# Four edits in one kernel: y stored from another queue, a new order of the first loads, a last block in two passes, and banded scores on row halves

## The chip, the cores and the metric

The kernel runs on one core of a Trainium2 chip. The time is the device time of one execution in microseconds (us). The engines of the core work in parallel, each through its own list of instructions, and meet at semaphores: TensorE (PE in the profile, its weight loads PEld), VectorE (DVE), ScalarE (ACT), GpSimd (POOL), and SyncE (SP), which here only issues transfers. PE's results land in eight PSUM banks; everything else is in SBUF.

## What is computed

A sequence of 512 tokens with 2048 channels goes through three layers, all in 32-bit floating point:

```python
# layer 1: forgetting attention, 32 heads of 64, full causal
p = rmsnorm(x) @ fox_w_in ; y = softmax(q k^T * scale + c_i - c_j) v ; x += (y * silu(gate)) @ fox_w_out
# layer 2: sliding window attention, 32 query heads, 4 key heads, window 128, one sink per head
p = rmsnorm(x) @ swa_w_in ; y = softmax over a band of two 128-key blocks ; x += (y * silu(gate)) @ swa_w_out
x = rmsnorm(x, final_g)
# layer 3: half of the channels through an RWKV-7 scan (16 heads of 64), half through HGRN-2 (8 heads of 128)
proj = x @ w_in_2 ; y = concat(o_rwkv, o_hgrn) @ w_out_2
out = layer_norm(ALPHA * x + y, ln_w, ln_b)
```

In the band, block b of 128 queries sees the 128 keys of its own block and the 128 of the block before it; block 0 has only its own.

## The kernel before

**Products.** Every large product is a list of blocks b of 512 output columns. A block needs 16 tiles of 128 input channels (kt); the weights come in slots of two kt, 8 slots in a block, 512 KB each. `products` (L243) issues for each kt and each of four banks j three matmuls (high x high, low x high, high x low, since each number is split in two parts), so a block is 192 matmuls of 512 columns. SP loads slot s into one of `NR` = 5 buffers once `w_free` says that slot s-4 has begun; ACT makes the high part (`split_act`, L523) into one of `NH` = 3 buffers, DVE the low part (`split_dve`, L674), both two slots ahead of PE. DVE takes a finished bank out and counts up `bank_free[j]`, for which the next block waits at its first kt.

**Side work.** The rest of the layers is woven between the matmuls of `products` at numbered points (4 kt + j, 64 in a block). The other engines hold the matching pieces in the same order, slot by slot, behind the split of the slot.

**The start.** SP issues six small constants (L1886), on which PE, ACT and DVE all wait, then weights and the transposed input xt in turn (L890, L891). POOL issues at once the gains, `w_f`, small parameters, cos and sin, and 1 MB of x (L899 to L906). ACT and DVE wait for four of POOL's parameters, and for xt in pairs of slots (`x_in`, 32 counts for two transfers).

**Sliding window scores.** `swa_scores` (L423) runs in each of 64 steps (4 groups g of 16 steps k; k is a head pair and a query block b = k % 4). For each of the two heads e it issues one fp32 matmul of the 128 rows of q of both heads against `kzs[:, e]`, in which the rows of the other head are zero, and then adds the mask by a bf16 matmul (`identb`, `maskb`). Both heads of a step share one bank, and steps alternate between two (`S_BANK`). DVE takes the row maxima of both heads in one reduction (L759), then L760 and L762; ACT takes the exponentials (L559) and that of the sink (L563); DVE divides (L768 to L770); PE turns the result (`swa_turn`, L449) in the next step and multiplies by v (`swa_values`, L460) in the one after. Steps are 5.8 points apart, in the last group 4 (`swa_step_at`).

**RWKV and HGRN units.** Layer 3 has 8 RWKV and 8 HGRN units. The product blocks alternate between them, and the side work of a unit runs under the blocks behind it. `hg_take` (L1623) takes HGRN unit h out of the banks into `hqs, hf, hi_, hz`; the y of the unit before it, in `hz_split` and `hkdtm_split` of the same memory, must by then have been stored in DRAM (`y_h_st`), and its last step is the subtraction L1711 (`y_h_lo`). POOL makes both stores (L1832, L1833), in a list sorted by the place at which each is due, together with the stores of RWKV's y (L1828, L1829) and with `sub_inverses` (L1789 to L1811): the inverses of 16 x 16 blocks by way of DRAM, at whose end POOL waits until `xt` has landed. In that list the stores of HGRN units 3, 4 and 5 stand behind `sub_inverses` of RWKV units 5, 6 and 7. After the list POOL loads all of y back for the last product (L1841, L1842), and the last product's first matmul waits for it.

**The end.** The last product (`out`, four blocks n of 512 output channels over four token tiles t, one bank each) is followed on DVE by the sum (L1717), `bn_stats` (L1721), `bn_aggr` (L1753) and the reciprocal root for all four tiles, then tile by tile the scaling on ACT (L1462, 2048 columns), the product with `ln_w` and the sum with `ln_b` on DVE (L1760, L1761), and a 1 MB store by SP (L1773).

## Time and profile before

| | us |
|---|---|
| median of 3 runs | 3324.41 |
| lowest and highest | 3318.13, 3325.99 |
| the profiled execution | 3318.51 |
| its span in the trace | 3316.7 |
| PE busy (15418 matmuls) | 3090.8 (93%) |
| DVE busy | 1656.3 (50%) |
| ACT busy | 1177.3 (35%) |
| POOL busy | 207.3 (6%) |

PE is busy for 93% of the span, and the chain that ended last runs over PE for 81% of it. The kernel can become faster where PE waits, where its clock is granted at the lower level, at the two ends where PE has no work, or where PE has less to do. The granted clock of the whole execution is 0.973 of full speed. A start in the trace is the instruction's own; a matmul's end is modelled, so the cost of a few matmuls is read from starts: from the last large matmul ahead of them to the second one behind them, less the two steps of 0.227 us that these take anyway.

### The profile page before, as it was taken

The numbers are of one execution on the slowest core, as the hardware profiler recorded it, in microseconds if no ns is written. First come the engines' busy times: TensorE is split into PE (matmuls) and PEld (weight loads), VectorE is DVE, ScalarE is ACT, GpSimd is POOL, SyncE is SP. The second block draws the span as 40 slices with busy tenths as digits, with TensorE's granted clock in tenths as the row PEclk, the third lists the DMA queues.
The fourth block names the chain that finished last, engine by engine and source line by source line (L and its number), as shares of the span: only waits on it lengthen the run. The fifth ranks groups of instructions, "written<-read, shape, count | busy, mean of one in ns | idle before, by whom it ended". The sixth has DMA issues, their size and how long they took to land.

```text
span 3316.7 us, 38969 instructions
## 1 busy us (share of the span) xinstructions
PE 3090.8 (93%) x15418; PEld 2468.4 (74%) x15418; DVE 1656.3 (50%) x2769; ACT 1177.3 (35%) x2056; POOL 207.3 (6%) x445
## 2 busy tenths in 40 slices
PE   7999999999999999999999999999999696978896
PEld 5777777777778887777778767878778485857685
DVE  5444444444433336556543455665656354544545
ACT  4333333333332324334333334343434242434421
POOL 0000000000000000000000010120202101010200
PEclk9999999999999999999999999999999798998998
DMA  4222222222234322222143322222222212121632
GB/s 154 73 81 73 80 74 79 75 78 76 78 100 136 108 83 71 64 70 70 53 150 128 107 78 68 66 87 69 80 71 71 65 58 65 58 66 51 203 127 89
DMA packets 83250, 284.68 MB, mean 86 GB/s; under 512 B 10864, under 2 KB 11504, under 8 KB 82304
## 3 DMA queue, kind: packets, MB, share of 16 engines
q1 hardware_dynamic: 63936, 232.13, 21.9%
q0 software_dynamic: 19136, 50.08, 4.7%
q8 instruction: 124, 2.03, 0.3%
q14 instruction: 54, 0.44, 0.0%
HBM read 256.93 MB, written 25.17 MB: 85 GB/s over the span
## 4 chain that ended last, share of the span: by engine, by line
PE 81%; DVE 9%; ACT 3%; issue 3%; DMA 2%; POOL 1%; SPq 0%; DVEq 0%; ACTq 0%; POOLq 0%
PE bank L257 14%; PE bank L259 13%; PE bank L258 13%; PE bank L261 7%; PE bank L263 7%; PE bank L262 7%; PE bank L281 2%; PE bank L1255 2%; PE bank L433 1%; PE bank L1191 1%; PE bank L1186 1%; PE bank L310 1%; ACT mc_split L523 1%; PE bank L460 1%; PE bank L449 1%
## 5 line engine op out<-in xcount | busy, mean ns | idle before, releaser
L257 PE MATMUL bank<-ma_split,mc_split 128*128 128x512 f32 x2304 | 964.2, 418 | 99.2 <-DVE mb L1623 68.6
L674 DVE TENSOR_TENSOR mc_split<-mc,mc_split 128x1024 fp32r<-128x1024 f32 x426 | 521.8, 1225 | 869.6 <-ACT mc_split L523 868.4
L259 PE MATMUL bank<-ma_split,mc_split 128*128 128x512 f32 x2304 | 909.2, 395 | 0.0
L258 PE MATMUL bank<-ma_split,mc_split 128*128 128x512 f32 x2304 | 906.9, 394 | 0.0
L523 ACT ACTIVATE mc_split<-mc 128x1024 fp32r<-128x1024 f32 x426 | 451.2, 1059 | 999.1 <-PE bank L257 599.1
L257 PEld LDWEIGHTS bank<-ma_split,mc_split 128*128 128x128 f32 x2304 | 439.5, 191 | 219.6 <-issue 125.5
L259 PEld LDWEIGHTS bank<-ma_split,mc_split 128*128 128x128 f32 x2304 | 437.5, 190 | 97.6
L258 PEld LDWEIGHTS bank<-ma_split,mc_split 128*128 128x128 f32 x2304 | 440.0, 191 | 78.7 <-issue 4.7
L261 PE MATMUL bank<-mc_split,ma_split 128*128 128x512 f32 x576 | 231.1, 401 | 3.2 <-DMA ma_split<-y 3.0
L263 PE MATMUL bank<-mc_split,ma_split 128*128 128x512 f32 x576 | 225.6, 392 | 0.0
L262 PE MATMUL bank<-mc_split,ma_split 128*128 128x512 f32 x576 | 225.3, 391 | 0.0
L261 PE MATMUL bank<-mc_split,mb_split 128*128 128x512 f32 x512 | 202.4, 395 | 3.5 <-DVE mc L882 2.8
L263 PE MATMUL bank<-mc_split,mb_split 128*128 128x512 f32 x512 | 200.3, 391 | 0.0
L262 PE MATMUL bank<-mc_split,mb_split 128*128 128x512 f32 x512 | 199.8, 390 | 0.0
L532 ACT ACTIVATE mc<-bank,stat 128x128 f32<-128x128 f32 (+3 forms) x128 | 67.5, 528 | 309.9 <-DVE stat L682 309.5
L261 PEld LDWEIGHTS bank<-mc_split,ma_split 128*128 128x128 f32 x576 | 108.9, 189 | 25.9 <-issue 5.3
L263 PEld LDWEIGHTS bank<-mc_split,ma_split 128*128 128x128 f32 x576 | 108.7, 189 | 23.4
L262 PEld LDWEIGHTS bank<-mc_split,ma_split 128*128 128x128 f32 x576 | 109.1, 189 | 20.9
L559 ACT ACTIVATE mc<-bank,stat 128x256 f32<-128x256 f32 (+1 forms) x128 | 56.1, 443 | 166.2 <-DVE stat L760 166.1
L261 PEld LDWEIGHTS bank<-mc_split,mb_split 128*128 128x128 f32 x512 | 96.4, 188 | 24.4 <-issue 3.7
L263 PEld LDWEIGHTS bank<-mc_split,mb_split 128*128 128x128 f32 x512 | 96.4, 188 | 20.5
L262 PEld LDWEIGHTS bank<-mc_split,mb_split 128*128 128x128 f32 x512 | 96.5, 188 | 19.1
(360 smaller groups left out, 3660.0 us busy)
## 6 DMA issues: line engine op xcount, KB each, us to landing
mc<-in_w SPq DMA_DIRECT2D x426, 512.0 KB, 3.5
x<-mc POOLq DMA_DIRECT2D x8, 1024.0 KB, 5.4
y<-mb_split POOLq DMA_DIRECT2D x28, 256.0 KB, 2.6
ma_split<-y POOLq DMA_DIRECT2D x28, 256.0 KB, 8.3
mb<-in_xt SPq DMA_DIRECT2D x8, 512.0 KB, 12.2
mc<-in_x POOLq DMA_DIRECT2D x4, 1024.0 KB, 6.0
mc<-x POOLq DMA_DIRECT2D x4, 1024.0 KB, 7.2
mats<-mc POOLq DMA_DIRECT2D x32, 128.0 KB, 2.2
```

Source lines behind the costliest of these rows:

```text
L257: mm = pe.matmul(banks[j][:], wh[:, c], act_hi[:, kt, :], start=(kt == 0), stop=False)
L258: pe.matmul(banks[j][:], wl[:, c], act_hi[:, kt, :], start=False, stop=False)
L259: last = pe.matmul(banks[j][:], wh[:, c], act_lo[:, kt, :], start=False, stop=(kt == KT - 1))
L261: mm = pe.matmul(banks[j][:], act_hi[:, kt, c], wh, start=(kt == 0), stop=False)
L262: pe.matmul(banks[j][:], act_hi[:, kt, c], wl, start=False, stop=False)
L263: last = pe.matmul(banks[j][:], act_lo[:, kt, c], wh, start=False, stop=(kt == KT - 1))
L281: pe.matmul(bank[:, 0:nk], qz[:, e, b * P:(b + 1) * P], kz[:, e, 0:nk], start=True, stop=False)
L523: act.activation(w_high[:, s % NH, :, :], w_raw[:, s % NR, :, :], ACT.Copy).then_inc(w_hi, 1)
L532: act.activation(prob[:, n % 2, 0:nk], S_BANK[n % 2][:, 0:nk], ACT.Exp, bias=nmax[:, k:k + 1], accum_out=rsum[:, k:k + 1]).then_inc(p_exp, 1)
L559: ins = act.activation(sprob[:, n % 2, e, 0:nk], S_BANK[n % 2][:, 2 * P * e:2 * P * e + nk], ACT.Exp, bias=nmax2[:, i + e:i + e + 1], accu ...
L674: dve.tensor_tensor(w_low[:, s % NR, :, :], w_raw[:, s % NR, :, :], w_high[:, s % NH, :, :].bitcast(F32), ALU.subtract).then_inc(w_lo, 1)
L1255: mm = pe.matmul(to[:, c], lhs[:, c * P:(c + 1) * P], frm[:, c], start=True, stop=True)
```

## The change

- **Stores of y.** POOL's list loses the HGRN stores. SP makes them (L1856, L1857 of the changed kernel), each pair five slots behind the place of L1711, between two weight loads, with a wait for `y_h_lo` in front. POOL's reload of y counts semaphores for two tiles at a time.
- **The start.** SP issues weights and xt first and the six constants behind them. Only work that needs the constants waits for them. The gains have a semaphore of their own, POOL's other loads wait until the third xt transfer has landed, each xt transfer has a semaphore, a dummy activation loads ACT's table, and the second split stands behind the first two kt.
- **The last block in two passes.** The last block's 8 slots are loaded and split twice: first all 16 kt for token tiles 0 and 1, then again for 2 and 3. The matmuls are the same 192. Sum, statistics, root, scaling and `ln_w` of tiles 0 and 1 are placed in the second pass. Scaling, products and stores go by halves of 1024 columns; the sum with `ln_b` is POOL's for tiles 0 to 2 and DVE's for tile 3.
- **Scores.** `kzs` has one plane, with head 0 in rows 0 to 63 and head 1 in rows 64 to 127, and is not zeroed. Every even step issues the scores of two query blocks: for each block the two masks, then one matmul per head of 64 rows. Each head has its bank, each block half of it. DVE's maxima go by head, for both blocks at the even step; `p_exp` is waited for without the slack of one step.

```diff
             def swa_scores(pe, g, k):
-                n, p, b = UNITS0 + 16 * g + k, k // TT, k % TT
-                k0, nk = keys(b)
-                bank = S_BANK[n % 2]
...
-                else:
-                    pe.wait_ge(p_exp, n - 1)
-                for e in range(2):
-                    pe.matmul(bank[:, 2 * P * e:2 * P * e + nk], qt[:, p, b * P:(b + 1) * P], kzs[:, e, k0:k0 + nk],
-                              start=True, stop=False)
-                    mm = pe.matmul(bank[:, 2 * P * e:2 * P * e + nk], identb[:], maskb[:, 2 * P - nk:2 * P],
-                                   start=False, stop=True)
-                mm.then_inc(s_done, 1)
+                pe.wait_ge(p_exp, n)
+
+                def to(b, e):
+                    return S_BANK[e][:, 2 * P * (b % 2):2 * P * (b % 2) + keys(b)[1] - keys(b)[0]]
+
+                for b in (k % TT, k % TT + 1):
+                    k0, k1 = keys(b)
+                    for e in range(2):
+                        pe.matmul(to(b, e), identb[:], maskb[:, 2 * P - k1 + k0:2 * P], start=True, stop=False)
+                    for e in range(2):
+                        hs = slice(e * HD, (e + 1) * HD)
+                        pe.matmul(to(b, e), qt[hs, p, b * P:(b + 1) * P], kzs[hs, k0:k1], start=False, stop=True
+                                  ).then_inc(s_done, 1)
...
-                if k < 16:
+                if k < 16 and k % 2 == 0:
                     swa_scores(pe, g, k)
...
             def second_sp(sp):
+
+                ends = {SLOT0[LANE0] + hg_at(h, HG_M - 1) // 8 + 5: h for h in range(UNITS - 1)}
...
                 for s in range(SLOT0[RW0], TOTAL_SLOTS):
+                    h = ends.get(s)
+                    if h is not None:
+                        sp.wait_ge(y_h_lo, h + 1)
+                        sp.dma_start(a["y2"][0, UNITS + h].bitcast(F32), hkdtm_split.bitcast(F32)).then_inc(y_h_st, 16)
+                        sp.dma_start(a["y2"][1, UNITS + h].bitcast(F32), hz_split.bitcast(F32)).then_inc(y_h_st, 16)
                     sp.wait_ge(w_free, s - NR + 2)
...
                 ends = sorted([(rw_at(u, RW_K - 1), 0, u) for u in range(UNITS - 1)]
-                              + [(hg_at(h, HG_M - 1), 1, h) for h in range(UNITS - 1)]
                               + [(rw_at(u, CHUNKS), 2, u) for u in range(UNITS)])
...
+                    if b == BLOCKS - 1:
+                        for half in range(2):
+                            for _ in products(pe, b, False, h_hi, h_lo, needs, SLOT0[b] + half * BLOCK_SLOTS,
+                                              range(2 * half, 2 * half + 2)):
+                                pass
                         continue
...
+                        if s >= BLOCK_SLOTS:
+                            if s == BLOCK_SLOTS:
+                                out_take(dve, st, n, b, (0, 1))
+                            if s == BLOCK_SLOTS + 1:
+                                norm_stats(dve, st, 0)
+                            if s in (BLOCK_SLOTS + 4, BLOCK_SLOTS + 6):
+                                norm_times(dve, (s - BLOCK_SLOTS - 4) // 2)
+                            continue
...
+            def norm_pool(pool):
+                pool.wait_ge(ln_in, 32)
+                for t in range(TT - 1):
+                    for half in range(2):
+                        c = slice(half * D // 2, (half + 1) * D // 2)
+                        pool.wait_ge(ln_times, 2 * t + half + 1)
+                        pool.tensor_tensor(x3[:, t, c], x3[:, t, c], ln_b[:, c], ALU.add).then_inc(ln_ready, 1)
...
             def first_pool(pool):
-                pool.dma_start(gains_t[:], a["gains_t"]).then_inc(par_in, 16)
+                pool.dma_start(gains_t[:], a["gains_t"]).then_inc(gains_in, 16)
+                pool.wait_ge(x_in[2], 16)
```

How the instructions stand before and after, at three places. (`mc` holds q, k, probabilities and weights; `bank` is any PSUM bank; xN repeats a row.)

PE before, at one step of the first sliding window group, for a query block with 256 keys; L433 are the scores, L435 the masks, L460 the values and L449 the turns:

```order
L433 MATMUL bank<-mc 128x256
L435 MATMUL bank<-maskb,identb 128x256
L433 MATMUL bank<-mc 128x256
L435 MATMUL bank<-maskb,identb 128x256
L460 MATMUL bank<-mc 64x128 x4
L449 MATMUL bank<-ident,mc 128x128 x4
```

PE in the changed kernel, at the even step that follows (blocks 0 and 1 of the next head pair); L446 are the masks, L449 the scores, L473 the values, L462 the turns:

```order
L446 MATMUL bank<-maskb,identb 128x128 x2
L449 MATMUL bank<-mc 128x128 x2
L446 MATMUL bank<-maskb,identb 128x256 x2
L449 MATMUL bank<-mc 128x256 x2
L473 MATMUL bank<-mc 64x128 x4
L462 MATMUL bank<-ident,mc 128x128 x4
```

The scores of two steps stand together, the odd step has only values and turns, and PE goes twice from masks on all 128 rows to scores on row halves.

POOL before, at the end of `sub_inverses` of RWKV unit 5; L1811 loads the inverses, L1832 and L1833 store HGRN unit 3's y, L1828 and L1829 RWKV unit 4's, L1789 begins the next `sub_inverses`:

```order
L1808 DMA inv<-mc 64x16x16
L1811 DMA mc<-inv 128x8x128
L1832 DMA y<-mb_split 128x512
L1833 DMA y<-mb_split 128x512
L1828 DMA y<-mb_split 128x512
L1829 DMA y<-mb_split 128x512
L1789 DMA mats<-mc 128x2x128 x4
```

SP in the changed kernel, in the same part of the program; L1859 are the weight loads, L1856 and L1857 the stores of HGRN's y:

```order
L1859 DMA mc<-in_w 128x1024 x16
L1856 DMA y<-mb_split 128x512
L1857 DMA y<-mb_split 128x512
L1859 DMA mc<-in_w 128x1024 x16
L1856 DMA y<-mb_split 128x512
L1857 DMA y<-mb_split 128x512
```

Each pair has moved from behind a whole `sub_inverses` on POOL to its place between weight loads on SP.

DVE before, behind the last product (all four token tiles):

```order
L1717 TENSOR_TENSOR mb<-bank,mb 128x512 x4
L1721 BN_STATS mc<-mb 128x6 x4
L1753 BN_AGGR mc<-mc 128x2 x4
L1755 RECIPROCAL mc<-mc 128x4
L1756 SCALAR_TENSOR_TENSOR mc<-mc 128x4
L1760 TENSOR_TENSOR mb<-mb,mc 128x2048
L1761 TENSOR_TENSOR mb<-mb,mc 128x2048
```

DVE in the changed kernel, behind the second pass; L1843 are the halves of the product with `ln_w`, L1828 those of the sum with `ln_b`, and the row L1843 x2 at the top, for tile 1, stands still under the second pass:

```order
L1843 TENSOR_TENSOR mb<-mb,mc 128x1024 x2
L1777 TENSOR_TENSOR mb<-bank,mb 128x512 x2
L1781 BN_STATS mc<-mb 128x6 x2
L1833 BN_AGGR mc<-mc 128x2 x2
L1835 RECIPROCAL mc<-mc 128x2
L1836 SCALAR_TENSOR_TENSOR mc<-mc 128x2
L1843 TENSOR_TENSOR mb<-mb,mc 128x1024 x4
L1828 TENSOR_TENSOR mb<-mb,mc 128x1024 x2
```

Behind the last matmul DVE has half of the statistics and, of eight passes of 2048 columns, what makes up three.

## Rows read from the trace of the kernel before

**Rows 1.** The page, its first part: busy time of each engine.

```profile
PE 3090.8 (93%) x15418; PEld 2468.4 (74%) x15418; DVE 1656.3 (50%) x2769; ACT 1177.3 (35%) x2056; POOL 207.3 (6%) x445
```

**Rows 2.** The waits of PE: line, releaser, us in total, times, longest.

```profile
PE bank L257 <- DVE mb L1623: 68.6, 4, 27.1
```

**Rows 3.** Timelines of several engines, 2610 to 2681: start, us, what, idle before.

```profile
2609.95 0.72 POOL L1789 DMA_DIRECT2D mats<-mc  x1
...
2614.80 0.68 DVE L1711 TENSOR_TENSOR mb_split<-mb,mb_split 128x512 fp32r<-128x512 f32 x1
...
2644.11 0.57 POOL L1832 DMA_DIRECT2D y<-mb_split  x1 [3.96 <-DMA mc<-inv]
...
2647.32 2.48 DVE L1623 TENSOR_TENSOR mb<-bank,mc 128x512 f32<-128x512 f32 x4 [29.09 <-DMA y<-mb_split]
...
2648.15 0.76 PE L257 MATMUL bank<-ma_split,mc_split 128*128 128x512 f32 x1 [27.06 <-DVE mb L1623]
...
2680.17 1.04 PE L1181 MATMUL bank<-ident,mc 128*128 128x128 f32 x8
```

**Rows 4.** Windows: us, busy of PE, PEld, DVE, ACT, POOL, then PEclk, DMA share, GB/s.

```profile
2650.00:2653.00 3.00, 3.00 (x11) 2.41 (x10) 1.66 (x2) 2.97 (x6) 0.00 (x0) 0.50 0.50 173
```

**Rows 5.** Timeline of PE at the first matmul of the last product.

```profile
3079.06 0.47 PE L261 MATMUL bank<-mc_split,ma_split 128*128 128x512 f32 x1 [2.99 <-DMA ma_split<-y]
```

**Rows 6.** The start: the chain's longest piece, then timelines of PE and ACT.

```profile
4.99 11.76 DMA mb<-in_xt
...
18.49 0.76 PE L257 MATMUL bank<-ma_split,mc_split 128*128 128x512 f32 x1 [18.49 <-DVE ma_split L809]
...
26.82 1.06 ACT L523 ACTIVATE mc_split<-mc 128x1024 fp32r<-128x1024 f32 x1 [2.12 <-DMA mc<-in_w]
```

**Rows 7.** The chain in order of time, at a sliding window step with 256 keys.

```profile
1505.02 0.43 PE bank L433 x2
...
1506.11 0.59 PE bank L460 x8
```

**Rows 8.** Timeline of PE, at a step with 128 keys (block 0).

```profile
1511.58 0.38 PE L433 MATMUL bank<-mc 128*128 128x128 f32 x2
...
1512.28 0.67 PE L460 MATMUL bank<-mc 128*64 128x128 f32 x8
```

**Rows 9.** Timeline of PE: matmuls on 64 rows between large ones, two places.

```profile
1937.39 0.39 PE L259 MATMUL bank<-ma_split,mc_split 128*128 128x512 f32 x1
1937.71 1.13 PE L1166 MATMUL bank<-mc 64*128 64x256 f32 x8
...
1939.11 0.40 PE L258 MATMUL bank<-ma_split,mc_split 128*128 128x512 f32 x1
...
2407.50 0.39 PE L259 MATMUL bank<-ma_split,mc_split 128*128 128x512 f32 x1
2407.82 1.12 PE L1132 MATMUL bank<-mc 64*128 64x512 f32 x2
...
2409.21 0.39 PE L258 MATMUL bank<-ma_split,mc_split 128*128 128x512 f32 x1
```

**Rows 10.** Timeline of DVE: maxima and division of the step of rows 7.

```profile
1506.14 0.69 DVE L759 TENSOR_REDUCE stat<-bank 128x2 f32<-128x512 f32 x1 [1.20 <-PE bank L435]
...
1508.68 0.69 DVE L770 TENSOR_TENSOR mc<-mc,stat 128x512 f32<-128x512 f32 x1
```

**Rows 11.** Timelines behind the last matmul, of PE, ACT and DVE.

```profile
3286.59 0.39 PE L263 MATMUL bank<-mc_split,ma_split 128*128 128x512 f32 x1
...
3290.60 0.63 DVE L1753 BATCH_NORM_AGGREGATE mc<-mc 128x2 f32<-128x24 f32 x4
3292.01 8.05 ACT L1462 ACTIVATE mb<-mb,mc 128x2048 f32<-128x2048 f32 x4 [0.45 <-DVE mc L1756]
...
3310.12 2.29 DVE L1761 TENSOR_TENSOR mb<-mb,mc 128x2048 f32<-128x2048 f32 x1
```

**Rows 12.** Timeline of POOL: its widest operation.

```profile
2629.37 0.30 POOL L1802 TENSOR_TENSOR mc<-mc 64x64 f32<-64x64 f32 x1
```

208 lines of the change are left out of this document (129 added, 79 removed).

## The prediction, made before the changed kernel was run

> **What bounds the kernel now.** I read the page first: PE is busy for 3090.8 of 3316.7 us [rows 1], so the reader should look for what keeps PE from working, and for work of PE that the change takes away. The table of PE's waits comes second: one row stands out, 68.6 us in 4 waits for L1623, the longest 27.1 [rows 2]; the waits at the other two long places are 23.1 and 17.1, and the fourth is 1.3. The timeline at the longest shows why: the y of HGRN unit 3 is ready at 2614.80 + 0.68 = 2615.5, POOL has been in `sub_inverses` since 2609.95 and issues the store at 2644.11, DVE waits 29.1 us for it, and PE begins its next block at 2648.15 after 27.1 us [rows 3]. Third come the two ends: PE starts at 18.49 [rows 6], and its last matmul starts at 3286.59 and ends near 3287.0, so that 29.7 us of the span lie behind it [rows 11].
>
> **HGRN's y from SP.** The stores are asked for at 2615.5 instead of 2644.1. They take two issues and some 2.5 us to land (DVE went on 3.2 us after POOL's issue [rows 3]), so they are in DRAM near 2618.7 to 2619.3. PE's last matmul of the block started at 2620.7 (27.06 and its own 0.39 before 2648.15 [rows 3]), the first bank is ready three banks earlier, near 2619.1, and DVE has three banks' time to empty it. So nothing, or some tenths, is left of the wait. The other two units have the same order of events. Gain: 27.1 + 23.1 + 17.1 = 67.3 us; the fourth wait of 1.3 I leave. Behind each long wait the granted clock is 0.50, the lower of its levels 1.2 and 2.4 GHz [rows 4], and PE had stood idle before it fell; PE then worked 5.4, 3.9 and 5.0 us at half speed, half of which is lost: 7.1 us. Sum 74.4. What is late next: the inverses for the same unit. They landed at 2644.1 and PE asked for them at 2680.2 [rows 3]; without 27.1 and 2.7 us it asks at 2650.4, 6 us of cover. The other two have about as much. SP's queue: each wait for `y_h_lo` stands in front of a weight load that has four slots, 21.8 us, until its matmuls, so a wait of a few us costs nothing. Bounds: 60 (stores queue behind a 512 KB load, some 3 us at each of three places) to 76.
>
> **The reload of y.** PE waits 3.0 us for it at the last product [rows 5], since POOL stood at unit 6's store first. Now POOL reloads tiles as the block before frees them. The half clock behind that wait lasts about 3 us more. Together 4.6 us. But soon behind it PE has to wait for DVE's chain of the last HGRN unit, which moves with the take of that unit and not with PE. I take 3; bounds 0 and 4.6.
>
> **The start.** The chain is a transfer: xt is issued at 4.99 and landed at 16.75 [rows 6], behind constants on SP and against POOL's 1 MB of x.  Now SP's first weight load goes out at about 0.75 instead of 3.6, one xt transfer is enough instead of two, and POOL is silent. At 0.34 MB a us (7.3 MB of weights, xt and x from about 5.5 until the fourth weight slot is in at 26.8 [rows 6]) the first two 0.5 MB transfers are in at about 4.6 and 6.1. Then 0.7 us for the high part, 0.8 for the low one and 0.2 of semaphores: PE starts at 7.9, 10.6 earlier. Not all stays: the fourth weight slot was landed at 26.8 [rows 6] with the same bytes ahead of it, and only 1.8 us come off. PE needs it, split (2.6 us), at 7.9 + 18.0 = 25.9 for the first six kt (3.6 us at half speed), and gets it at 25.0 + 2.6 = 27.6, with one more kt to make behind it on ACT and DVE. So about 2 us are given back. Gain 8.5; bounds 5 and 11.
>
> **The end.** Before, behind the matmuls: 3.6 us to L1753, 1.4 to the first scaling, 2.2 of it, then eight passes of 2.29 at 2.28 from start to start, and 4.3 us from 3312.4 for the last store [rows 11]. Now: two sums and two statistics end 2.2 us behind the last matmul, aggregates, root and reciprocal 1.1, the first half scaled 1.05 (2.01 for 2048, [rows 11]); DVE then has four half products and two half sums, 6 x 1.15 = 6.9; the last 0.5 MB store 3.5. Sum 14.8, against 29.7: gain 14.9. POOL's half sums have no row of their size. From below they cost 1.15 (DVE's); from above, by its 64 elements in 0.30 [rows 12], 4.8. I take 2.4, nearer to the lower end, since an operation of 64 elements is for the most part its start: tile 2's sums then end near 10.3, before DVE's. At 4.8 POOL would end at about 21 and the gain would be 5 to 6. The second loads of the last block ask for 0.5 MB every 2.72 us, 0.19 MB a us; 0.34 was seen. The splits need 1.06 and 1.23 us of each 2.72. Neither costs anything. Bounds 5 and 16. The Trainium skill, GPSIMD Reference, section 3.1, has 4497 ns for a `tensor_tensor` of 2048 fp32, which as an estimate from that page is 2.2 for a half; its section 8 warns that POOL shares SBUF interfaces with DVE's two-input instructions. No row here has both at work at this size; by it the gain would be 1 to 3 us smaller.
>
> **Scores on row halves.** Before, a step with 256 keys costs PE 1506.11 - 1505.02 = 1.09 us [rows 7], of which 0.86 are the four passes of the scores and 0.22 the masks; with 128 keys it is 0.70 [rows 8]. Four matmuls of 256 columns on alternating row halves cost (1939.11 - 1937.39) - 2 x 0.227 = 1.27 us [rows 9], where one after another they would be 1.72: the halves do run together. But a single matmul of 512 columns on one half costs 1.26 [rows 9], though its columns are worth 0.86. So going into the half rows and out again costs 0.4, and four scores in pairs 0.87. The trace shows this price at every such place (29 groups of L1166, between 1.27 and 1.32 where nothing waited). A pair of scores is then 0.44, a change of row mode 0.2. A pair of blocks with 256 keys: 2 x (0.22 + 0.44) + 3 added changes x 0.2 = 1.92, before 2.18. Blocks 0 and 1: 0.20 + 0.44 + 0.22 + 0.44 + 0.6 = 1.90, before 1.79. With 16 of each: 4.2 less, 1.8 more, 2.4 us gained. The Trainium skill, TensorEngine Tiling (Array Packing), says in its table of theoretical speedups that a contraction of 64 or less gives up to 2x, and in Key Properties that changing the tiling mode drains the engine. Of the first, the trace shows the 0.87 for 1.72; of the second, the 0.4.
>
> Against this stands a longer way round. DVE waits for both blocks, then has four reductions, each with a semaphore, and two pairs of small operations. A reduction of 512 columns takes 0.69 [rows 10], one of 256 by estimate 0.42: 2.5 us to the last maximum instead of 0.9. ACT and DVE then need what they did: from the scores' end at 1506.1 to the end of L770 at 1508.68 + 0.69 = 1509.4, 3.3 us [rows 10], so 4.9 now. PE comes back to the turn 1.2 + 4.0 + 0.8 = 6.0 us behind its scores in the first three groups, 4.7 in the last. There 8 pairs lose some tenths each, and where a split (1.23) of DVE falls between, up to 1 us anywhere. I take 5 us in 32 pairs, with 0 and 30 as ends. Net 2.6 slower.
>
> **Sum.** 74.4 + 3 + 8.5 + 14.9 - 2.6 = 98 us off the profiled execution's 3318.5: 3220. The median of the runs is 3324.4, 5.9 above it; I put the forecast half way, 3223.
>
> **Rivals.**
> (a) Changes of row mode hide behind weight loads. For it: masks and scores lie next to each other, no large matmul is among them. Against: both places of rows 9 show the price. PE would save 32 x 3 x 0.2 = 19 us more: 3204.
> (b) The longer way round makes PE wait in most pairs, about 1 us, and now and then the clock falls: 30 us instead of 5, so 3248.
> (c) Stores and POOL are late: HGRN stores queue behind weight loads, the inverses become the next wait, or POOL's sums are slow. Each is 5 to 20 us: 3245 to 3260. Against it are the 6 us of cover and the 21.8 us of SP.
> (d) SP's wait for `y_h_lo` stops the weights: slower than before. It decides when L1711 is done more than 21.8 us behind the place of the wait. To eat 98 us, each of seven would have to be 36 us late. The trace has L1711 5 us ahead of the block's end; nothing speaks for it: above 3330.
> (e) SP's stores do not come earlier, because DVE reaches L1711 later once nothing holds it: the 67 us stay, 3295.
>
> **How the numbers follow.** Forecast 3223: 0.60. (a) 0.12, (b) 0.12, (c) 0.10, (d) 0.02, (e) 0.04. Leaving out (d), (e) and the upper part of (c) and of (b) gives 3198 to 3248. A measurement of this kernel tells 0.3%, 10 us, from no change. All cases but (d) are faster by more: faster 0.97, same 0.01, slower 0.02.
>
> **What the profile of the changed kernel would show.** No wait of over 2 us of PE for the first take of an HGRN unit, and no clock of 0.50 behind it; PE's first matmul at 7 to 9; 13 to 17 us behind the last one; each even step's scores at 1.8 to 2.0 us by starts, 1.3 if (a) holds; PE's waits for DVE's division under 10 us in sum. I am wrong if the first inverse's transpose waits for its transfer, if POOL's sums end behind DVE's, or if the sliding window stage grows or shrinks by over 10 us.

## The result, and the profile after

The median of the changed kernel's runs is 3231.0 us (3226.4 to 3234.7), that of the kernel before, on the same chip, 3323.0. The ratio is 0.9724, with a 95% interval from 0.9706 to 0.9742: 2.8% faster. The forecast was 3223 in a range from 3198 to 3248. The time is inside the range, 8 us above the forecast. The sum of the prediction, 3220, was for the profiled execution. That execution of the changed kernel took 3234.7 us with a span of 3232.9, which is 83.8 us less than the 3316.7 before.

The changed kernel was profiled a second time later (experiment 9 below), with a span of 3226.1. That is nearer to the medians, whose difference is 92 us, so both executions stand in the table of stages further down.

The page, its first part, to be read against [rows 1]:

```profile
PE 3079.9 (95%) x15418; PEld 2439.5 (75%) x15418; DVE 1673.4 (52%) x2844; ACT 1185.3 (37%) x2070; POOL 230.5 (7%) x437
```

PE has as many matmuls and is busy for 11 us less. The rest of the gain is time in which PE had stood idle, and it shows in its waits. The table of PE's waits: line, releaser, us in total, times, longest:

```profile
PE bank L1294 <- DVE mb L1702: 14.3, 4, 8.4
PE bank L261 <- DVE ma_split L837: 10.3, 2, 7.7
...
PE bank L1220 <- DMA mc<-inv: 8.0, 2, 5.2
...
PE bank L462 <- DVE mc L801: 5.3, 12, 1.0
PE bank L473 <- DVE mc L593: 2.8, 4, 0.7
...
PE bank L261 <- DVE mb L1683: 1.3, 1, 1.3
```

The first row to look for is the last one: L1683 is L1623 of before, and of 68.6 us [rows 2] only 1.3 are left. Two rows have come up. PE waits 8.0 us for the transfer of the inverses, where it waited 0.3 before, and 5.3 us in twelve small waits for DVE's division (L801). A third has grown: the first row is this one of before, and its longest wait went from 6.3 to 8.4 us:

```profile
PE bank L1255 <- DVE mb L1642: 12.1, 4, 6.3
```

The wait of [rows 5] for the reload of y has no row any more.

The timeline at the place of [rows 3], one unit of HGRN after the change (DVE, SP's queue, and DVE again):

```profile
2605.20 0.67 DVE L1771 TENSOR_TENSOR mb_split<-mb,mb_split 128x512 fp32r<-128x512 f32 x1
2605.89 0.33 SPq L1856 DMA_DIRECT2D y<-mb_split  x1
2606.26 0.43 SPq L1857 DMA_DIRECT2D y<-mb_split  x1
...
2609.77 2.48 DVE L1683 TENSOR_TENSOR mb<-bank,mc 128x512 f32<-128x512 f32 x4 [1.16 <-DMA y<-mb_split]
```

SP issues the first store as soon as L1771 ends. DVE waits 1.16 us instead of 29.09, and PE does not wait at all.

The start, timelines of PE and ACT, to be read against [rows 6]:

```profile
7.68 0.76 PE L261 MATMUL bank<-ma_split,mc_split 128*128 128x512 f32 x1 [7.68 <-DVE ma_split L837]
...
26.21 1.06 ACT L538 ACTIVATE mc_split<-mc 128x1024 fp32r<-128x1024 f32 x1 [11.47 <-DMA mc<-in_w]
...
29.33 0.47 PE L261 MATMUL bank<-ma_split,mc_split 128*128 128x512 f32 x1 [2.62 <-DVE ma_split L837]
```

PE starts at 7.68 instead of 18.49. The fourth weight slot is split at 26.21 instead of 26.82, and PE stands for 2.62 us before it can go on.

The end, timelines of PE, POOL, DVE and ACT, to be read against [rows 11]:

```profile
3212.63 0.39 PE L267 MATMUL bank<-mc_split,ma_split 128*128 128x512 f32 x1
...
3213.89 1.27 DVE L1777 TENSOR_TENSOR mb<-bank,mb 128x512 f32<-128x512 f32 x2
...
3216.53 0.39 DVE L1833 BATCH_NORM_AGGREGATE mc<-mc 128x2 f32<-128x24 f32 x2
...
3219.18 8.24 DVE L1843 TENSOR_TENSOR mb<-mb,mc 128x1024 f32<-128x1024 f32 x4 [1.38 <-ACT mb L1522]
3220.48 5.85 POOL L1953 TENSOR_TENSOR mb<-mb,mc 128x1024 f32<-128x1024 f32 x2 [2.70 <-DVE mb L1843]
3227.34 2.35 DVE L1828 TENSOR_TENSOR mb<-mb,mc 128x1024 f32<-128x1024 f32 x2
```

The last matmul ends at 3212.63 + 0.39 = 3213.0, and 19.9 us of the span lie behind it, against 29.7 before. Four half products take 8.24 us and two half sums beside them on POOL 5.85.

**By stages.** Outside the sliding window scores the traces have the same order of matmuls, so the start of each large matmul in one can be set against the start of the same one in the other. The lanes are the stage of the RWKV and HGRN units, and the long takes are the three of [rows 2]. The difference is flat within a stage and steps where something changed. This is worked out from PE's timelines; a minus is time gained.

| stage (us of before) | forecast | changed | changed, second execution |
|---|---|---|---|
| start, to 60 | -8.5 | -5.5 | -5.6 |
| 60 to 1890, the sliding window stage in it | +2.6 | -4.4 | -4.3 |
| the lanes up to the first long take | 0 | +0.3 | +0.2 |
| the three long takes | -74.4 | -29.9 - 25.0 - 19.7 = -74.6 | -74.6 |
| behind the takes (inverses, HGRN's levels) | 0 | +13.2 | +6.4 |
| reload of y | -3 | -3.6 | -3.6 |
| last block to the last matmul | 0 | +0.6 | +0.7 |
| behind the last matmul | -14.9 | -9.8 | -9.8 |
| sum | -98 | -83.8 | -90.6 |

The takes came out to a fifth of a microsecond. What is missing is at the start, behind the takes and at the end, and the sliding window stage gave more than was asked of it. Of the 13.2 us behind the takes 2.4 are at the grown wait for L1702, behind the third of them; the others are at the inverses.

### The profile page after: what moved, and what is told of

It reads as the page before. It is cut to its first block, busy times and chain, and to the rows that moved or that the text cites. A ratio compares the mean times of both kernels' runs of the same rounds, so it can differ in the third digit from the quotient of the medians.

```text
span 3232.9 us, 39162 instructions
## 1 busy us (share of the span) xinstructions
PE 3079.9 (95%) x15418; PEld 2439.5 (75%) x15418; DVE 1673.4 (52%) x2844; ACT 1185.3 (37%) x2070; POOL 230.5 (7%) x437
## 4 chain that ended last, share of the span: by engine, by line
PE 79%; DVE 11%; ACT 4%; issue 2%; DMA 2%; POOL 1%; SPq 0%; DVEq 0%; ACTq 0%; POOLq 0%
PE bank L261 14%; PE bank L263 13%; PE bank L262 13%; PE bank L265 7%; PE bank L267 7%; PE bank L266 7%; PE bank L285 2%; PE bank L1294 2%; ACT mc_split L538 1%; PE bank L1230 1%; PE bank L1225 1%; DVE mc_split L694 1%; PE bank L314 1%; PE bank L449 1%; PE bank L294 1%
## 5 line engine op out<-in xcount | busy, mean ns | idle before, releaser
L694 DVE TENSOR_TENSOR mc_split<-mc,mc_split 128x1024 fp32r<-128x1024 f32 x434 | 533.6, 1230 | 860.9 <-ACT mc_split L538 859.3
L538 ACT ACTIVATE mc_split<-mc 128x1024 fp32r<-128x1024 f32 x434 | 459.5, 1059 | 911.4 <-PE bank L261 512.1
L266 PEld LDWEIGHTS bank<-mc_split,ma_split 128*128 128x128 f32 x576 | 108.9, 189 | 20.7
```

Of the source, the lines that this page charges most:

```text
L266: pe.matmul(banks[j][:], act_hi[:, kt, c], wl, start=False, stop=False)
L538: act.activation(w_high[:, s % NH, :, :], w_raw[:, s % NR, :, :], ACT.Copy).then_inc(w_hi, 1)
L694: dve.tensor_tensor(w_low[:, s % NR, :, :], w_raw[:, s % NR, :, :], w_high[:, s % NH, :, :].bitcast(F32), ALU.subtract).then_inc(w_lo, 1)
```

## The experiments

Each was compared with the kernel before on its chip, and read by the same stages.

### 1. The stores of HGRN's y alone

```diff
--- the kernel before
             def second_sp(sp):
+                ends = {SLOT0[LANE0] + hg_at(h, HG_M - 1) // 8 + 5: h for h in range(UNITS - 1)}
                 for s in range(SLOT0[RW0], TOTAL_SLOTS):
+                    h = ends.get(s)
+                    if h is not None:
+                        sp.wait_ge(y_h_lo, h + 1)
...
-                              + [(hg_at(h, HG_M - 1), 1, h) for h in range(UNITS - 1)]
...
```

> The kernel before with one part of the change: SP stores HGRN's y (of units 0 to 6). Theory A (the stores' gain comes as forecast, but POOL's chain of inverses runs slower once DVE works beside it, 17 us instead of 11 between its first and last small operation, and the inverses become the next wait): the three long waits of 27.1, 23.1 and 17.1 us for the take of an HGRN unit go, PE waits 2 to 6 us at two or three places for the transfer of the inverses, and the execution is 58 to 64 us shorter than before (ratio 0.981). Rival B (the forecast's term stands and the inverse waits in the changed kernel come from its other parts): no wait of over 1 us for the inverses, 73 to 76 us shorter (ratio 0.977). Rival C (most of the gain of the changed kernel is from elsewhere): under 50 us shorter.

Measured: ratio 0.9792 (0.9769 to 0.9814), and a profiled span of 3254.7, 62.0 us under before. Two rows of PE's waits:

```profile
PE bank L1181 <- DMA mc<-inv: 5.6, 3, 2.8
PE bank L257 <- DVE mb L1623: 1.3, 1, 1.3
```

Theory A holds: three quarters of the whole gain are this one part, and it brings the wait for the inverses with it, and the wait of 8.4 us for L1642 (6.3 before) too. POOL's chain between its first and last small operation is 16.9 and 15.9 us long for the units that had 10.7 and 10.7 before. The theory's band of 58 to 64 us was met in part by something that it did not have. The three takes alone gave 75.0 us, and 7.5 went at the waits behind them; but 7.8 more were lost ahead of the first take, 2.7 of them at a wait of 1.96 for the inverses of the unit before, the rest in steps of 1.0 to 1.6 us, each with more of the lower clock than the kernel before has there.

### 2. All sums of the end on DVE

```diff
--- the changed kernel
                     dve.tensor_tensor(x3[:, t, c], x3[:, t, c], ln_w[:, c], ALU.mult).then_inc(ln_times, 1)
+                    if t < TT - 1:
+                        dve.wait_ge(ln_times, 2 * t + half + 1)
+                        dve.tensor_tensor(x3[:, t, c], x3[:, t, c], ln_b[:, c], ALU.add).then_inc(ln_ready, 1)
...
-                norm_pool(pool)
```

> The changed kernel, but DVE also makes the sums with ln_b of tiles 0 to 2, in halves, right behind each product; POOL has nothing to do at the end. Theory A (POOL and DVE hold each other up when both have two inputs of 1024 columns in SBUF: DVE's half product took 3.0 us instead of 1.15 in the trace): products and sums take 1.15 each, DVE takes the first bank of the last pass within 1 us of its matmul instead of 3.9, the end behind the last matmul shrinks from 22.9 to 17 to 18 us, and the execution is 5 to 6 us shorter than the changed kernel's. Rival B (the long products come from something else, the second loads or the splits on DVE's own queue): the products stay near 3 us, DVE has six half sums more, and the kernel is 2 to 8 us slower.

The 22.9 us in this expectation, and in those of experiments 6 and 8, were counted from 3210.04, where the last run of twelve matmuls begins; from the end of the last matmul they are 19.9. Measured: ratio 0.9748 (0.9729 to 0.9767). The timeline of DVE at the end:

```profile
3225.33 1.23 DVE L1843 TENSOR_TENSOR mb<-mb,mc 128x1024 f32<-128x1024 f32 x1 [1.38 <-ACT mb L1522]
3226.59 1.22 DVE L1846 TENSOR_TENSOR mb<-mb,mc 128x1024 f32<-128x1024 f32 x1
3227.73 1.22 DVE L1843 TENSOR_TENSOR mb<-mb,mc 128x1024 f32<-128x1024 f32 x1
```

The half products are back at 1.15 to 1.25 from start to start, as theory A has it, so that what made them long was POOL. But the gain did not follow: the last matmul ends at 3218.6 and the span at 3238.0, 19.4 us behind it, 0.5 less than with POOL's help. DVE now has eight halves of 1.18, 9.4 us, for the 10.5 before, and it takes the first bank 1.6 us behind the last matmul instead of 0.9, since the sums of tile 1 stand ahead of it. And 0.7 us are lost just before the last matmul, where PE waits 1.05 us for DVE's last split instead of 0.3. The rest of the profiled execution's 5 us over the changed kernel is upstream, in places that the edit does not touch. So POOL's help is worth about nothing, neither a loss nor a gain.

### 3. Weights between the xt transfers

```diff
                 for i in range(KT // 2):
-                    if i < 3:
+                    if i < NR:
                         sp.dma_start(w_raw[:, i, :, :], a["w1"][i].rearrange("p (k n) -> p k n", k=2)).then_inc(w_full[i], 16)
...
-                for s in range(3, SLOT0[RW0]):
+                for s in range(NR, SLOT0[RW0]):
```

> The changed kernel, but SP issues weight slots 3 and 4 between the xt transfers, and the constants behind all of them. Theory A (the fourth weight slot was late only because 5.9 MB were ahead of it): it lands near 13 to 16 us instead of 26.2, PE does not wait and its clock does not fall between 26 and 34 us, and block 1 starts 5 us earlier than in the changed kernel: 5 us shorter in all. Rival B (outstanding transfers share the bandwidth, so that what goes out earlier for weights comes later for xt): the fourth slot is early but an xt transfer is late instead, PE waits for that, and the gain is 0 to 2 us.

ACT's timeline at the fourth slot:

```profile
16.54 1.06 ACT L538 ACTIVATE mc_split<-mc 128x1024 fp32r<-128x1024 f32 x1 [1.58 <-PE bank L261]
```

The slot is split at 16.54, when its buffer comes free, and no longer waits for its transfer. PE has no second wait, the clock does not fall there, and the first blocks are 4.1 us earlier than in the changed kernel's first execution. Theory A holds for the start, but one execution does not give its size. The start without this edit stands in seven traces, and its second wait there is 1.5 to 3.9 us. In experiment 7, whose edit is far behind the start, the slot is split at 24.69, the wait is 1.50, the clock does not fall, and the first blocks are already 3.1 us earlier. Against the changed kernel's first execution the seven lie between 1.1 us later and 3.1 earlier, 0.4 earlier in the mean, and the three with this edit (experiments 3, 8 and 10) 4.1, 5.2 and 4.3 us earlier: the edit is worth about 4 us. The ratio, 0.9737 (0.9718 to 0.9756), shows nothing of it: 1.6 us are gone again at 915 and 2.9 near 2690, each with falls of the clock that the changed kernel's profile does not have there, and 1 more by 2900.

### 4. Two changes of row mode in place of four

```diff
-                for b in (k % TT, k % TT + 1):
-                    k0, k1 = keys(b)
-                    for e in range(2):
-                        pe.matmul(to(b, e), identb[:], maskb[:, 2 * P - k1 + k0:2 * P], start=True, stop=False)
-                    for e in range(2):
-                        hs = slice(e * HD, (e + 1) * HD)
-                        pe.matmul(to(b, e), qt[hs, p, b * P:(b + 1) * P], kzs[hs, k0:k1], start=False, stop=True
-                                  ).then_inc(s_done, 1)
+                for e in range(2):
+                    mask(b0, e, start=True, stop=False)
+                for e in range(2):
+                    score(b0, e, start=False, stop=True).then_inc(s_done, 1)
+                for e in range(2):
+                    score(b1, e, start=True, stop=False)
+                for e in range(2):
+                    mask(b1, e, start=False, stop=True).then_inc(s_done, 1)
```

`mask` and `score` are the two matmuls of the changed kernel; `b0` and `b1` are the pair's blocks.

> The changed kernel, but in each pair of blocks the second block's masks stand behind its scores (masks, scores of both blocks, masks), so that PE goes into row halves once instead of twice. By starts a pair now costs 1.51 us (blocks 0 and 1) and 1.82 us (2 and 3) in the changed kernel, about 0.5 more than its columns are worth. Theory A (0.13 us for each change of row mode, four of them): both fall by 0.26 us, 8 us in 32 pairs; PE comes back earlier to the turns and waits for DVE's division more, so the stage gets 3 to 8 us shorter. Rival B (0.2 for each change, as forecast): both fall by 0.4, up to 13 us. Rival C (the 0.5 are not from changes of row mode): within 0.05 us a pair of what they cost now.

PE's timeline in the changed kernel, around the scores of blocks 2 and 3:

```profile
1220.30 0.39 PE L263 MATMUL bank<-ma_split,mc_split 128*128 128x512 f32 x1
1220.53 0.39 PE L446 MATMUL bank<-maskb,identb 128*128 128x256 bf16 x2
1220.85 0.70 PE L449 MATMUL bank<-mc 64*128 64x256 f32 x4
1221.48 0.39 PE L446 MATMUL bank<-maskb,identb 128*128 128x256 bf16 x2
1221.81 0.70 PE L449 MATMUL bank<-mc 64*128 64x256 f32 x4
...
1223.53 0.39 PE L262 MATMUL bank<-ma_split,mc_split 128*128 128x512 f32 x1
```

and in this experiment:

```profile
1222.62 0.39 PE L263 MATMUL bank<-ma_split,mc_split 128*128 128x512 f32 x1
1222.86 0.39 PE L445 MATMUL bank<-maskb,identb 128*128 128x256 bf16 x2
1223.18 1.14 PE L450 MATMUL bank<-mc 64*128 64x256 f32 x8
1224.24 0.39 PE L445 MATMUL bank<-maskb,identb 128*128 128x256 bf16 x2
...
1225.66 0.39 PE L262 MATMUL bank<-ma_split,mc_split 128*128 128x512 f32 x1
```

The group costs 1223.53 - 1220.30 - 0.45 = 2.78 us in the one and 1225.66 - 1222.62 - 0.45 = 2.59 in the other. At blocks 0 and 1 it is 2.69 and 2.49. Two changes of row mode are gone for 0.20 us, so one costs 0.10: nearer to theory A's 0.13 than to rival B's and the forecast's 0.2, and rival C is out. Over the stage PE's starts come 5.8 us nearer, of 32 x 0.20 = 6.4 on PE, and PE's waits for DVE grow from 8.1 to 9.3. The profiled span is 3224.8, 8.1 less than the changed kernel's first; the ratio is 0.9725 (0.9704 to 0.9746), so the runs do not tell the difference.

### 5. The inverses in two transfers

```diff
...
-                                pe.wait_ge(xt_in, 16 * (u + 1))
+                                pe.wait_ge(xt_in2 if p else xt_in, 16 * (u + 1))
...
-                pool.dma_start(xt, mats(a["inv"])).then_inc(xt_in, 16)
+                pool.dma_start(xt[:, 0:4, :], mats(a["inv"])[:, 0:4]).then_inc(xt_in, 16)
+                pool.dma_start(xt[:, 4:8, :], mats(a["inv"])[:, 4:8]).then_inc(xt_in2, 16)
...
```

> The changed kernel, but POOL's load of the inverses is issued as two transfers of 256 KB with a semaphore each, and PE's first four transposes wait for the first alone. Theory A (PE's waits of 2.8 and 5.2 us for the inverses are the tail of POOL's chain, whose last link is one 512 KB transfer of 5 to 6 us): the first half lands 1.5 to 2.5 us earlier, so the waits shrink to 0.5 to 1.3 and 2.7 to 3.7 us, 3 to 5 us in sum with one or two drops of the clock less. Rival B (the transfer time is queueing behind weights and not its size): the waits stay within 0.5 us.

Ratio 0.9724 (0.9708 to 0.9741). At the two places PE's first transposes start 3.5 us behind POOL's issue instead of 4.8 and 6.2. At the first it then waits twice, 1.48 and 1.43 us, for 2.81 before: nothing won. At the second it does not wait for the first half and 0.49 for the second, but the second execution of the unedited kernel waits only 0.99 there. So the first half is there 1.3 us sooner than the whole, a little less than theory A's 1.5 to 2.5, and at the first place PE then waits for the second half. Neither theory holds as written, and the time shows nothing.

### 6. POOL's sum and DVE's product in turn

```diff
                     dve.wait_ge(ln_scaled, 2 * t + half + 1)
+                    if 0 < 2 * t + half < 7:
+                        dve.wait_ge(ln_ready, 2 * t + half)
```

> The changed kernel, but each half product of DVE from the second on (to the first half of tile 3) waits until POOL's sum of the half before it has ended, so that the two never work on these at once. It measures the disputed operation by itself. Theory A (POOL's sum took 2.9 us only because it alternated with DVE's product, and DVE's 1.15 became 3.0 by waiting for it): alone the half product takes 1.15 us and POOL's half sum 1.9 to 2.4. Rival B (POOL needs 2.9 us for 1024 columns alone too, and DVE's product still waits for the whole of it when they meet): product 1.15, sum 2.8 to 3.0. In either case the end behind the last matmul is longer than 22.9 us, 23 to 27, since DVE now waits for each.

The timeline of DVE and POOL:

```profile
3205.93 1.23 DVE L1845 TENSOR_TENSOR mb<-mb,mc 128x1024 f32<-128x1024 f32 x1 [2.25 <-POOL mb L1955]
3207.07 1.22 DVE L694 TENSOR_TENSOR mc_split<-mc,mc_split 128x1024 fp32r<-128x1024 f32 x1
3207.23 2.91 POOL L1955 TENSOR_TENSOR mb<-mb,mc 128x1024 f32<-128x1024 f32 x1 [1.41 <-DVE mb L1845]
...
3211.58 2.00 POOL L1955 TENSOR_TENSOR mb<-mb,mc 128x1024 f32<-128x1024 f32 x1 [1.44 <-DVE mb L1845]
```

Alone, POOL's half sum takes 2.00 us, and DVE's half product 1.23. Where a split of DVE (3207.07 to 3208.29) runs when the sum begins, the sum takes 2.91: about its own 2.00 behind the 1.06 from 3207.23 until the split has ended. Theory A is shown, rival B is out. It takes an operation of DVE with two inputs in SBUF: in the changed kernel a half sum of POOL from 3215.79 on runs beside `bn_stats` (0.69 us, one input) and takes 1.99. Behind the last matmul lie 23.2 us, or 26.2 from where the expectation counts, inside its 23 to 27. The kernel was executed once, so this is not a comparison of times.

### 7. Three of POOL's fifteen steps

```diff
...
-                for k in range(SUB - 1):
+                for k in range(3):
...
```

> The changed kernel, but POOL makes 3 of the 15 steps of the substitution for the inverses, so it leaves out 12 multiplications and 12 sums per unit (and the inverses are not the inverses). It asks what POOL's chain costs PE in all. Theory A (the chain is what PE waits for behind HGRN's take in the changed kernel, 2.8 + 5.2 us, and the clock falls there): both waits go, POOL's chain is 13 us shorter, the execution 8 to 13 us shorter. Rival B (what PE would wait for next is just behind, as the level of HGRN with its wait of 8.4 us): the waits move to that, and the execution is under 4 us shorter.

Ratio 0.9705 (0.9687 to 0.9724), median 3223.5. PE's table of waits has no row for the inverses any more, and PE's starts around the two places gain 11.9 us on the first execution of the changed kernel and 5.2 on the second. The row of 8.4 us for L1702 stays. The chain costs PE 5 to 12 us, and with the 2.4 us at L1702 that is about what the stages show behind the takes, 6.4 and 13.2. The rest of the profiled gain of 11.6 us is not the edit's: 3.1 came at the start and went again by 2460. By medians the gain is about 6 us, and the intervals overlap. Both waits are gone and no other has grown, as theory A has it; its 8 to 13 us fit the first execution of the changed kernel alone.

### 8 and 10. Four edits together, twice

The edits of experiments 2, 3, 4 and 5, with the scaling of tiles 0 and 1 a slot earlier and their products two.

```diff
-                            if s in (BLOCK_SLOTS + 4, BLOCK_SLOTS + 6):
-                                norm_times(dve, (s - BLOCK_SLOTS - 4) // 2)
+                            if s in (BLOCK_SLOTS + 2, BLOCK_SLOTS + 4):
+                                norm_times(dve, (s - BLOCK_SLOTS - 2) // 2)
```

> The changed kernel with four edits: weight slots 3 and 4 between the xt transfers, masks of the second block behind its scores, inverses loaded in halves, and at the end all sums on DVE with the scaling of tiles 0 and 1 one slot earlier and their products two slots earlier. By stages, if each keeps what it showed alone: 4 us at the start (it showed 4.1 up to the first RWKV block), 5 to 6 in the sliding window stage, 3 to 5 at the inverses, 4 to 5 at the end (19.8 to about 18 behind the last matmul, from 22.9): 16 to 20 us shorter than the changed kernel, 3213 to 3217. Rival: the time gained ahead of the RWKV and HGRN lanes is lost in them again by drops of the clock (the run with the earlier weights lost all of its 4 us there): 3220 to 3225.

> The four edits together a second time, timed on the same chip in the same call as the changed kernel. By stages the first run gained 5.2 us at the start, 5 in the sliding window stage and 5.2 at the end, and drops of the clock took some back. Theory A (edits keep their gains, drops are chance): 10 to 16 us under the changed kernel's median of this call, ratio to the kernel before 0.968 to 0.970. Rival B (what is gained ahead of the two lanes is lost in them, as a rule): 3 to 8 us under it, 0.970 to 0.972.

Measured: 0.9706 (0.9691 to 0.9722), span 3225.6, and 0.9707 (0.9686 to 0.9729), span 3216.7. On the chip of the second one the changed kernel had 0.9726 (0.9705 to 0.9746): medians of 3224.2 and 3228.9, 4.8 us. That lies in rival B's band for experiment 10. By stages the two executions gain 5.2 and 4.3 us at the start and 5.7 each in the sliding window stage, and lose 1.5 each at 915. Behind the last matmul they gain 2.6 each, 17.3 us for 19.9. But the end as a whole gains nothing, since 3.1 and 3.2 us are lost shortly before the last matmul: the products and sums of tiles 0 and 1, placed earlier on DVE, hold up a split, and PE waits for it. PE's timeline in experiment 8:

```profile
3198.26 0.47 PE L265 MATMUL bank<-mc_split,ma_split 128*128 128x512 f32 x1 [1.81 <-DVE mc_split L704]
```

The lanes take back 1.5 us in the first execution, which spends 17 us more of them at the lower clock than the second; in the second they gain 8.3, where the second execution of the changed kernel has 6.8 without any edit. So neither theory holds as a rule. The intervals overlap: this is the fastest version, by some 5 us, but the runs do not settle it.

### 9. The changed kernel again

> The changed kernel itself a second time. The stages of all kernels so far, laid beside each other by PE's starts, differ by steps of 1.6 us at places that no edit touches (at 915 us in six of them, not in the changed kernel's first execution), each with one more or one less short fall of the granted clock to 0.50. Theory A (whether the clock falls at such a place differs from execution to execution of the same program): this profile shows steps of 1.6 us, up or down, against the first one, at two to six places, with no change in the waits of over 1 us. Rival B (each program has its own places, set by its code): no such step, and PE's starts agree within 0.5 us from the first block to the last product.

The two executions agree within 0.3 us up to 2780 us, with the same falls of the clock: rival B so far. Then they part, at the transfers of one unit. POOL's load of the inverses and PE's first transpose, in the first execution and then in the second:

```profile
2783.18 0.91 POOL L1906 DMA_DIRECT2D mc<-inv  x1 [4.36 <-DMA inv<-mc]
2789.36 1.97 PE L1220 MATMUL bank<-ident,mc 128*128 128x128 f32 x8 [5.22 <-DMA mc<-inv]
```

```profile
2780.43 0.91 POOL L1906 DMA_DIRECT2D mc<-inv  x1 [2.79 <-DMA inv<-mc]
2785.14 1.09 PE L1220 MATMUL bank<-ident,mc 128*128 128x128 f32 x8 [0.99 <-DMA mc<-inv]
```

POOL's store of the inverses was issued at 2777.96 and then at 2776.77, since the store ahead of it, of the blocks, had landed 1.0 us sooner. The store of the inverses took 4.36 us of waiting and then 2.79, the load 6.2 and then 4.7 until PE began. These are the 1.2, 1.6 and 1.5 us between the waits. The wait is 5.22 in one and 0.99 in the other, and only behind the longer one does the clock fall. The window of the first execution (us, busy of PE, PEld, DVE, ACT, POOL, then PEclk, DMA share, GB/s):

```profile
2789.00:2796.00 7.00, 6.63 (x31) 6.06 (x31) 0.00 (x0) 2.12 (x4) 0.00 (x0) 0.59 0.01 2
```

That is 4.2 us of wait and 2.6 at half clock, 6.8 in all, between two executions of the same program.

## Why the prediction was right, and where it was not

**HGRN's y from SP: right, and to the size.** 74.6 us for the 74.4 of the sum, and 75.0 in experiment 1, which has it alone.

**What is late next: wrong.** The prediction saw the inverses coming and gave them 6 us of cover. The step that failed is the length of POOL's chain, taken to stay as it was. It was read at [rows 3], where DVE stood idle for 29 us, waiting for the very store that the change moves. Without that wait DVE works, and POOL's operations wait for it. Two pairs in the changed kernel's timeline:

```profile
2618.88 1.23 DVE L694 TENSOR_TENSOR mc_split<-mc,mc_split 128x1024 fp32r<-128x1024 f32 x1 [1.70 <-ACT mc_split L538]
2618.94 1.29 POOL L1897 TENSOR_TENSOR mc<-mc 64x48 f32<-64x48 f32 x1
...
2620.02 0.77 DVE L1713 SCALAR_TENSOR_TENSOR mb<-mb,mc 128x512 f32<-128x512 f32 x1
...
2620.31 0.62 POOL L1900 TENSOR_TENSOR mc<-mc 64x48 f32<-64x48 f32 x1
```

An operation of 48 elements takes 1.29 us: it ends at 2620.23, behind DVE's at 2620.11. The next one takes 0.62 for the same reason, where its like takes 0.28. So the chain from the first to the last small operation is 17.0 and 16.1 us for the two units that wait, against 10.7 each before: 6.3 and 5.4 us. That alone is not the wait. POOL's last store of the blocks and its load of the inverses, before and after, at the first of the two:

```profile
2618.53 0.72 POOL L1789 DMA_DIRECT2D mats<-mc  x1 [2.48 <-DVE mc L1114]
...
2639.22 0.93 POOL L1811 DMA_DIRECT2D mc<-inv  x1 [2.78 <-DMA inv<-mc]
```

```profile
2608.92 0.72 POOL L1884 DMA_DIRECT2D mats<-mc  x1 [2.48 <-DVE mc L1153]
...
2638.94 0.93 POOL L1906 DMA_DIRECT2D mc<-inv  x1 [3.58 <-DMA inv<-mc]
```

That is 20.7 us and then 30.0, 9.3 longer: 6.3 in the operations and 3.0 in the small transfers between them. At the second unit it is 22.1 and then 30.0, 7.8 longer, 2.4 of them in transfers, and the load itself takes 1.6 more. The cover, without PE's wait and the half clock, was 6.6 us at the first and only 4.0 at the second, so "the other two have about as much" was a misreading too (the third had 16). What is left is 2.8 and 5.4 us, and PE waits 2.8 and 5.2. Why the transfers take longer is not shown. From 2634 to 2639 the DMA engines moved 13 GB/s before, while PE stood and no weights were asked for, and 118 after; but in the second execution of the changed kernel the small transfers of the second unit are only 0.2 us longer than before, so chance has a part in it. The trace of before had a row for the chain, had it been read at a unit whose DVE was at work. POOL there, first and last pair of the unit ahead of that of [rows 3]:

```profile
2490.86 0.20 POOL L1802 TENSOR_TENSOR mc<-mc 64x15 f32<-64x15 f32 x1 [3.71 <-DMA mc<-mats]
...
2507.87 0.30 POOL L1805 TENSOR_TENSOR mc<-mc 64x15 f32<-64x15 f32 x1
```

17.3 us, and 29.6 from the last store of the blocks to the load. With these 29.6 for the 20.7 and 22.1, the sum would have had waits of 2.3 and 3.5 us and some half clock: this is rival (c), which had 0.10 and came in part. Experiment 7 shows what the chain costs, 5 to 12 us.

**The start: the first step right, the second mis-sized.** PE began at 7.7, as forecast (7.9). The fourth slot was set at 25.0 and was there at 26.2, split at 28.5; PE waited 2.62 us, until 29.33, and then worked at half clock for 3.4 us:

```profile
28.00:36.00 8.00, 6.67 (x22) 5.36 (x23) 8.00 (x12) 7.97 (x13) 0.00 (x0) 0.79 0.25 77
```

The mean clock of 0.79 in these 8 us is 3.4 us at the lower level, 1.7 lost. Against before, PE's starts lose 0.8 us in the first twelve matmuls, which take 5.25 us instead of 4.51, 2.8 at that wait and 1.7 at half clock, so 5.3 of the 10.8 are given back, where the sum had 2.1. The term is the transfer: the slot was issued at 10.5 with all of xt ahead of it, and its split moved from 26.8 to 26.2, by 0.6 us, where the sum took 1.8. In experiment 7 it moved by 2.1, so that a part of this is chance. Experiment 3 shows what the order of two loads is worth, about 4 us. The result is within the step's bounds, 5 and 11, at their lower end.

**The end: mis-sized by 5.1 us, inside its bounds.** Term by term: sums and statistics end 3.5 us behind the last matmul instead of 2.2, since DVE came 0.9 late, behind a product that had waited for POOL; aggregates to the first scaled half took 2.7 for 2.15; DVE's halves took 10.5 for 6.9; the last store 3.2 for 3.5. The step that failed is "6 x 1.15 = 6.9". It took DVE's halves as if POOL were not there, and POOL's as something that only has to end in time. POOL's half sum was put at 2.4, between 1.15 and 4.8; alone it takes 2.00 (experiment 6). It is the meeting of the two that costs. The Trainium skill, GPSIMD Engine Reference, section 8, names this, interfaces of SBUF shared with DVE's instructions of two inputs, and the prediction set 1 to 3 us beside its sum for it: the trace agrees with the rule and has 3.6. Its section 3.1, halved, gave 2.2 us, an estimate from that page, for the 2.00 measured. Experiment 2 shows that taking POOL away wins only half a microsecond behind the last matmul, and loses 0.7 ahead of it; with the products placed earlier it is 2.6 won and 3.1 lost (experiments 8 and 10).

**Scores on row halves: the sign was wrong, by 7 us, well inside -19 and +30.** By starts the four steps of a head pair cost PE 8.17 us before and 7.62 now. The first and last pair of a group gain less, so over all 16 head pairs, waits left out, it is 7.3 us, where the sum had 2.4. Two sizes were off. A change of row mode costs 0.10, not 0.2 (experiment 4); the 0.4 of [rows 9] held two of them and something more, and no run tells what. And blocks 0 and 1 were given 0.44 for scores of 128 columns, the price of 256; they cost 1.51, not 1.90. The pair of 256 keys costs 1.82 (1.92 forecast). The other side of the term, the longer way round, was right: PE's new waits for DVE are 5.3 + 1.3 = 6.6 us against the 5 of the sum. A further 1.8 us of a wait at 1645 and one fall of the clock there (1.7) went away without being in the sum. These parts make 4.2 us. The sliding window stage by itself shows 4.2, so close by luck, since a wait costs PE's starts up to 0.14 us more than its idle time; the other 0.2 of the 4.4 in the table lie ahead of it. Rival (a), masks and scores that hide the change, is out, and (b), 30 us of waits, too. The stage shrank by 4 to 5 us, under the 10 that would have made the forecast wrong.

**The reload of y:** 3.6 us for 3.

**Signs that were to show it.** No wait of over 2 us for a take: 1.3. PE's first matmul at 7 to 9: 7.7. 13 to 17 us behind the last: 19.9, missed. Even steps' scores at 1.8 to 2.0 us: 1.5 and 1.8. Waits for the division under 10 us: 5.3. Of the three signs of being wrong one did show: the first transpose of the inverses waited for its transfer. POOL's sums ended at 3226.3, ahead of DVE's. Behind the takes, at the end and at the start 13 + 5 + 3 us of the 98 were taken back, and the scores gave 7. So the profiled execution is 14 us over the sum's 3220, with 21 us of errors one way and 7 the other, and the number is nearer than the terms by luck. Without these 7 the median would be 3238, still inside the range.

Rivals (d) and (e) had nothing: PE's table has no wait for a weight of the lanes, and L1771 at 2605.20 stands as far ahead of L1711's 2614.80 [rows 3] as all else at that place, 9.6 us.

## What to carry to other kernels

When a change takes a wait away, read the lengths of all that runs beside it where that wait does not stand: a chain on POOL timed while DVE was idle is the chain's best case, not its price. Before element-wise work is split between DVE and POOL, ask whether both have two inputs in SBUF at the same time; here two engines needed 10.5 us for what one does in 9.4. Work that is moved ahead of the last matmul can hold up what PE waits for there: 2.6 us were won behind it and 3.1 lost ahead of it. And of a load that is to come earlier, ask what is ahead of it in its own queue: the place of two loads was worth about 4 us at the start.

## What the runs showed that was not expected

- POOL's operation of two inputs, begun beside one of DVE's that has two inputs in SBUF, goes on until that one has ended and then takes its own time, and the other way round. POOL's half sum is 2.00 us alone and 2.91 beside a split; DVE's split of 1.22 us took 3.02 beside a sum, and its half product as long.
- A change of row mode on PE costs 0.10 us in masks and scores of 128 to 256 columns.
- One more fall of the clock to its lower level costs 1.3 to 1.7 us, and one wait that is 4 us longer can bring it. Two executions of the changed kernel had them at the same places until a transfer parted them; two of the kernel of experiment 8 did not, and differed by 9 us. So for an edit worth 2 to 5 us the stages of a trace tell what it does, where the medians of three to five rounds don't.
- The same 512 KB transfer of the inverses took 4.7 us once and 6.2 another time, from its issue to PE's start.
